# Eight small tiles placed in front of hhi and hlo, so that two activation tiles begin at another address

## The reference, cut to what matters

```python
h = rms_norm(x, norm1_w) * (1.0 + scale1) + shift1
proj = h @ w_in                                   # 1024 wide in: q, k, v, xBC, z, dt, gates
...
merged = g_attn * (attn @ w_attn_out) + g_ssd * (ssd @ w_ssd_out)
x = x + gate1 * (merged @ w_o)
h2 = rms_norm(x, norm2_w) * (1.0 + scale2) + shift2
x = x + gate2 * (square(relu(h2 @ w_mlp1)) @ w_mlp2)
# second block
u = rms_norm(h, norm1_w);  proj = u @ w_in
...
h = h + mix @ w_out
u2 = rms_norm(h, norm2_w)
h = h + (silu(u2 @ w_gate) * (u2 @ w_up)) @ w_down
```

## Time and profile before

| | |
|---|---|
| runs of the kernel before | 1010.43, 1007.97, 1009.35 us, median 1009.35 |
| profiled execution, span from the first to the last instruction | 1007.1 us |
| TensorE matmul busy, share of the span | 938.6 us, 93% |
| VectorE, ScalarE, GpSimd busy | 667.8, 511.2, 105.6 us |
| mean granted TensorE clock | 0.976 of full speed |
| bytes read from HBM | 166.73 MB, 167 GB/s over the span |

### The profile page before, as it was taken

How to read it: one execution, slowest core, us unless ns; L and a number is a source line. 1 busy time by engine, 2 the same in 40 slices (tenths; PEclk the granted TensorE clock), 3 DMA queues, 4 the chain that set the end, 5 groups by cost and what they waited for, 6 DMA issues and landing times.

```text
span 1007.1 us, 18347 instructions
## 1 busy us (share of the span) xinstructions
PE 938.6 (93%) x7516; PEld 904.7 (90%) x7516; DVE 667.8 (66%) x945; ACT 511.2 (51%) x696; POOL 105.6 (10%) x85
## 2 busy tenths in 40 slices
PE   4299999999987988998999999999998999999998
PEld 4299999888876878998999999989998989999998
DVE  5855899988489998775866644453675665555552
ACT  2365654666677666343545533344558544444431
POOL 0500155200124343000000000000000000000000
PEclk9999999999999999998999999989999989999999
DMA  9755344566411225474755555535241235555561
GB/s 344 271 202 187 126 168 162 212 212 209 169 58 68 84 85 187 172 263 172 251 189 171 197 183 193 177 124 190 85 156 54 93 120 190 184 175 201 176 209 35
DMA packets 25086, 168.81 MB, mean 168 GB/s; under 512 B 2868, under 2 KB 4532, under 8 KB 4920
## 3 DMA queue, kind: packets, MB, share of 16 engines
q1 hardware_dynamic: 23616, 164.64, 47.0%
q10 hardware_dynamic: 1400, 3.16, 0.8%
HBM read 166.73 MB, written 1.06 MB: 167 GB/s over the span
## 4 chain that ended last, share of the span: by engine, by line
PE 78%; DVE 8%; ACT 7%; issue 4%; POOL 1%; DMA 1%; POOLq 0%; SPq 0%; DVEq 0%; ACTq 0%
PE bank L1689 76%; ACT kw__113 L747 2%; DVE acc L1043 1%; DMA raw<-w_stream 1%; POOL sqs L467 1%; DVE wlo L1020 1%; ACT whi L532 1%; PE bank L1872 1%; DVE kw__113 L1292 1%; DVE eb L1283 1%; DVE hlo L1126 0%; DVE yt L1313 0%; DVE kw__113 L1299 0%; ACT zt L772 0%; ACT L724 0%
## 5 line engine op out<-in xcount | busy, mean ns | idle before, releaser
L1689 PE MATMUL bank<-hhi,whi 128*128 128x256 f32 (+1 forms) x1384 | 404.8, 292 | 11.9 <-DVE hlo L1126 6.8
L1020 DVE TENSOR_TENSOR wlo<-raw,whi 128x2048 fp32r<-128x2048 f32 (+1 forms) x131 | 300.6, 2295 | 159.3 <-ACT whi L532 159.1
L1689 PE MATMUL bank<-hlo,whi 128*128 128x256 f32 (+1 forms) x1384 | 397.3, 287 | 0.0
L1689 PE MATMUL bank<-hhi,wlo 128*128 128x256 f32 (+1 forms) x1384 | 397.1, 287 | 0.0
L532 ACT ACTIVATE whi<-raw 128x2048 fp32r<-128x2048 f32 (+1 forms) x132 | 250.2, 1896 | 90.6 <-PE bank L1689 65.5
L1689 PEld LDWEIGHTS bank<-hhi,whi 128*128 128x128 f32 (+1 forms) x1384 | 270.3, 195 | 19.6 <-issue 17.9
L1689 PEld LDWEIGHTS bank<-hlo,whi 128*128 128x128 f32 (+1 forms) x1384 | 270.7, 196 | 0.3
L1689 PEld LDWEIGHTS bank<-hhi,wlo 128*128 128x128 f32 (+1 forms) x1384 | 270.2, 195 | 0.0
L1689 PE MATMUL bank<-fhi,whi 128*128 128x256 f32 x432 | 121.1, 280 | 0.0
L1689 PE MATMUL bank<-fhi,wlo 128*128 128x256 f32 x432 | 120.5, 279 | 0.0
L1689 PE MATMUL bank<-flo,whi 128*128 128x256 f32 x432 | 120.5, 279 | 0.0
(11 more groups left out here) (274 smaller groups left out, 1293.1 us busy)
## 6 DMA issues: line engine op xcount, KB each, us to landing
raw<-w_stream SPq DMA_DIRECT2D x156, 1024.0 KB, 4.9
xres<-x_t ACTq DMA_DIRECT2D x1, 1024.0 KB, 10.0
out<-oute SPq DMA_DIRECT2D x8, 128.0 KB, 4.4
tabs<-tabs_in_dram ACTq DMA_DIRECT2D x1, 641.0 KB, 5.6
tabs<-tabs_in_dram ACTq DMA_DIRECT2D x1, 512.0 KB, 3.4
hankel<-bucket_rows ACTq DMA_DIRECT2D x1, 512.0 KB, 5.9
cols<-cols_in_dram ACTq DMA_DIRECT2D x1, 325.0 KB, 12.9
tabs<-tabs_in_dram ACTq DMA_DIRECT2D x1, 64.0 KB, 12.6
```

The lines of the kernel that those rows point to most:

```text
L1020: nc.vector.tensor_tensor(out=wlo[:, c % RING, 0:n], in0=raw[:, r % RING, 0:n], in1=whi[:, c % RING, 0:n].bitcast(f32), op=ALU.subtract)\
L1689: return nc.tensor.matmul(out, lhsT, rhs, start=start, stop=stop)
```

## The change

Eight small tiles (448 bytes of a partition together) stand in front of `hhi` in place of behind `tabs`. The diff is complete:

```diff
     raw = place("raw", [P, RING, CW], f32)
     whi = place("whi", [P, RING, CW], f32r)
     wlo = place("wlo", [P, RING, CW], f32r)
-    hhi = place("hhi", [P, KD, T], f32r)
-    hlo = place("hlo", [P, KD, T], f32r)
-    xres = place("xres", [P, KD, T], f32)
-    cols = place("cols", [P, NCOL], f32)
-    tabs0 = here[0]
-    tabs = place("tabs", [P, NTAB], f32)
     csil = place("csil", [P, KD], f32)
     mod = place("mod", [P, 48], f32)
     mscale = place("mscale", [P, 2 * KD], f32)
     root = place("root", [P, NT], f32)
     rcol = place("rcol", [P, NT], f32)
     qw8 = place("qw8", [P, 2], f32)
     epsc = place("epsc", [P, 1], f32)
     onec = place("onec", [P, 1], f32)
+    hhi = place("hhi", [P, KD, T], f32r)
+    hlo = place("hlo", [P, KD, T], f32r)
+    xres = place("xres", [P, KD, T], f32)
+    cols = place("cols", [P, NCOL], f32)
+    tabs0 = here[0]
+    tabs = place("tabs", [P, NTAB], f32)
     dtk = place("dtk", [P, NT, 2 * NH], f32)
```

## The result

The changed kernel took 991.55 us (median of four runs, 989.66 to 995.58), the kernel before 1009.15 us beside it (median of four runs, the fourth being 1008.96). The ratio is 0.9846, 95% interval 0.9817 to 0.9874: 17.6 us less, where 15.5 were forecast. The ratios here compare runs taken beside each other; the median of the kernel before differs from one set to the next (1006.59 to 1009.15 us).

What follows compares the result with a forecast made beforehand. TensorE, busy 93% of the span, was taken to bound the kernel by matmul spacing. Phase gains of 17.7 us, less 0.6 lost in m2 and 1.6 for waits and settling, gave 15.5 us: 1009.35 to 994 us, range 986 to 1004.

Steps and rivals of the forecast that it cites:

- The cause: Products streaming hhi or hlo: the streamed tile's address against the loaded weights sets the spacing, 120.0 against 113.3 or 117.8 ns.
- my slower rival: hhi at 576 modulo 1024, unlike the arena's 64, might lock at 122 ns: 1016 us; chance 0.05.
- The bounds of one product: Each hhi or hlo product on the chain gains 2.22 to 6.67 ns; 3,500 products give 7.8 to 23.3 us.
- Which of the two: How a series begins sets 113.3 or 117.8 ns until something interrupts; assigned by phase, the hhi gains sum to 17.7 us.
- one of my signs of being wrong: gu at 117.8 ns in the profile after: the entry rule, and with it the largest term, 6.9 us, would be wrong.
- the rival's 2.3: Slow arena spacing everywhere: all hhi products, gu included, at 117.8 ns; 1004.7 us, or 1002 if dn loses nothing; chance 0.17.
- The first term: First stretch (340 products) and z (336) begin behind many-column float32 matmuls: 113.3 ns, 4.5 us saved.
- m2 inherits: If m1 ends at 117.8 ns, m2's first 133 products probably stay there and lose 0.6 us.
- The other tiles cost nothing: Moving xres, cols and tabs costs nothing; if tabs mattered on some 300 matmuls, 1.8 us either way.
- a sign of being right: Profile after: hhi spacing 113.3 or 117.8 ns in m1 and gu, while ao, so and wo stay as before.
- What the saving meets: Other engines, tight VectorE in xbc (3.8 us slack) and settling runs take off 1.6 us; the weight stream has room.

Runs made afterwards that it cites:

- e2: Kernel before with dtk placed in front of hhi: hhi and hlo move 512 bytes but keep remainder 128 modulo 512; 1007.62 us, ratio 1.0005.
- e3: Changed kernel with raw, whi and wlo moved too, so weight rings, hhi, hlo and arena all begin at remainder 64; 1014.4 us, ratio 1.0072.
- e1: TensorE alone, both blocks left out: streamed pair at sixteen remainders, 0 to 480, weights at 128; 113.3 ns at 64, 120.0 at 128.
- e7: The changed kernel unaltered, run again on another chip run with a second profile; 988.54 us, ratio 0.9837, profiled execution 988.32 us.
- e4: Changed kernel with gsel and ngsel (64 bytes) between hhi and hlo: hhi stays at remainder 64, hlo at 128; 1003.43 us, ratio 0.9961.
- e8: Third placement, edited from the kernel before: wlo at remainder 0, hhi and hlo at 64 modulo 256, whi at 128; 980.95 us, ratio 0.9751.
- e5: TensorE alone, both blocks left out: streamed pair at remainders 32 to 92 in 4-byte steps, four entries each; only 64 reached 113.3 ns.
- e9: TensorE alone, both blocks left out: streamed pair at 64 or 192, wlo at 128 or 0, eleven entries each; 113.3 and 117.8 ns at the change's placement.
- e6: TensorE alone, both blocks left out: high tile, low tile and wlo at different remainders, 22 cases; 21 at 116.9 to 121.1 ns, one at 113.33.

## Why the prediction was right, step by step

**The cause: right, and sharper now.** I inferred from ao beside ga and gs that the streamed tile's address modulo 512 mattered relative to the weights. e2 and e3 show it: hhi at a new place but at distance 0 keeps 120.0 ns (e2), and dn, whose tile stays at its address while the weights move to distance 0, falls from 113.4 to 119.9 ns (e3). The period is 256 bytes (e1). "Modulo 1024", my slower rival, had no part: hhi at 576 behaves as fhi at 64.

The windows (e1, e3) show that a weight load and a streamed operand disturb each other by their addresses. The Trainium skill's page "SBUF — State Buffer", section "Who interferes with whom", has TensorE's two SBUF read ports independent and TensorE waiting on no one; by it none of these runs could differ. The measurement decides, and the spacing differs by 6% between distance 0 and the best. How the reads collide inside is not shown here.

**The bounds of one product: right.** 2.22 to 6.67 ns; in the long stretches with hhi nothing outside the arena's two spacings appeared. The parts that I then name add up to 3,559 products where the bounds use 3,500, which moves them by 0.1 and 0.4 us.

**Which of the two: wrong in part, and this was the uncertain term.** I had read the state off the kind of entry. It is not fixed by that: two executions of one program had gu in different states. I had expected 113.3 ns for gu because its clock rises within it. Three long stretches with hhi begin in this way, at 474, 667 and 816 us of before: in the first profile only the first of them was at 113.3 ns, in e7 all three. gu at 117.8 ns was one of my signs of being wrong, and the first profile shows it. Term by term, from the starts of the same matmuls in the profiles of before, of the change and of e7:

| stretch of before | forecast | first profile | e7 |
|---|---|---|---|
| 47 to 103 and 195 to 266 us | 4.5 | 1.3 | 1.1 |
| xbc, 103 to 172 us | 2.3 | 2.7 | 2.7 |
| 470 to 569.5 us (m1) and out2 | 1.9 | 2.7 and 0.5 | 2.4 and 1.1 |
| m2's first 15 us | -0.6 | -0.6 | -0.6 |
| in2, 673 to 752 us | 2.1 | 1.9 | 4.0 |
| gu | 6.9 | 2.3 | 6.9 |
| dn | 0 | -2.3 | 0.0 |
| sum | 17.1 | 8.5 | 17.6 |

gu's 6.9 us is exactly what e7 has, and the first profile has the rival's 2.3. m1 and xbc gained more than their terms, in2 in e7 alone, where about 0.8 of its 4.0 us is a shorter time at the lower clock. For m1 the reason is an oversight of mine: it is not one unbroken series. Eight one-column matmuls stand behind its fourth chunk, and the 192 products in front of them were at 113.3 ns, the 576 behind them at 117.8. The line of before:

```profile
499.53 0.95 PE L1689 MATMUL bank<-onec,acc 128*128 128x1 f32 x8
```

That the total came out close owes something to luck. The spans of the two profiles are 13.3 and 20.7 us shorter than that of before, and the table's stretches account for only 8.5 and 17.6 of them. The rest, 4.8 and 3.1 us, came from places where I had forecast nothing, and is told below. The medians are 17.6 and 19.0 us shorter than those beside them, the forecast was 15.5.

**The first term: sized too high.** I gave it 4.5 us and it brought 1.3 and 1.1. Some 190 products before 83 us went at 117.8 and not at 113.3 (0.8 us), z's runs of 24 gained 1.7 us in place of 2.2, and the clock took most of the rest. Windows from 95 to 104 us, of before and of the change:

```profile
95.00:104.00 9.00, 9.00 (x68) 0.81 0.27 107
```

```profile
95.00:104.00 9.00, 9.00 (x54) 0.62 0.24 97
```

The clock was at its lower level twice as long there (0.62 against 0.81 of full on the mean), which is 14 matmuls fewer in 9 us, 1.7 us. e7 has the same 0.62. Of the other placements e2, e4 and e8 have 0.81 as before, and e3 has 0.58. Whether this time belongs to the change is open. Over the whole span the mean granted clock of the first profile is the same as before, 0.976.

**m2 inherits: right. The other tiles cost nothing: wrong in part.** m2's start at 117.8 cost 0.6 us as worked out. I had not seen that the arena phases would change their states as well. m2 had 117.8 in all seven later stretches before. After, the stretches alternate, 113.3 in the first, third, fifth and seventh and 117.8 between them, alike in both profiles of the change. Windows of the first two, of the change:

```profile
578.30:588.30 10.00, 10.00 (x90) 1.00 0.60 211
590.00:600.00 10.00, 10.00 (x87) 1.00 0.62 210
```

This gave 1.4 us back, and the same in wo 0.4 us. ao alternates too, where all eight runs had been at 113.3, but it lies off the chain. I had named ao, so and wo staying as before as a sign of being right. In m2 the only tile that the change moved is `onec`, which the one-column matmuls between the stretches stream: from remainder 160 to 32 modulo 256. The profiles with onec at 160 and the weights at 128 (before, e2) have 117.8 in all seven, those with it at 32 (the change, e7, e4) alternate. So the move of onec is the likely cause; no run moved it alone.

The clock gave the rest, and that is not shown to come from the change. Between 774 and 789.5 us (attention of block 2) the granted clock was 0.89 before and 1.00 in both profiles of the change, 1.4 us. Another 1.6 us came around 400 us in the first profile. Windows of so's first matmuls, of before and of the change:

```profile
395.50:402.50 7.00, 7.00 (x49) 0.76 0.94 336
```

```profile
391.60:398.60 7.00, 7.00 (x63) 1.00 0.92 342
```

e7 has 0.76 there like before, with the same program as the first profile, so this part is luck of the execution. The runs of before beside e2 to e4 go from 1001.3 to 1010.6 us; that such differences of the clock make their spread is not shown.

**What the saving meets: right.** VectorE did not become the bound in xbc, the ring of three slots held gu at 113.3 ns, and 266 to 395 us is as long as before within 0.2 us. The other moved tiles cost VectorE and ScalarE nothing: VectorE's busy time is 667.2 against 667.8 us, ScalarE's 511.4 against 511.2.

## What to carry to other kernels

When the same product takes a different time from start to start with another tile, compare the addresses of its two operands, not the engines around it. Their addresses matter modulo 256 bytes, and every tile of the group must be at its place: here high and low activation at 64, whi at 128, wlo at 0. 4 bytes off, most or all of the gain is gone: 118.6 to 118.9 ns at 60 and 121.7 at 68, against 120.0 where nothing is moved and 113.3 at 64 (e5). Take more than one profile of such a kernel before a term is believed, since a phase of 1,000 matmuls may be in either of two states in the next execution. Follow every tile that a change moves, also those of the short matmuls between the long series.

## What the runs showed of the hardware that was not expected

- Three matmuls of 128 x 128 by 128 x 256 with their weight loads take 340, 353 or 360 ns in this kernel, by little more than the addresses of the tiles modulo 256 bytes; single remainders gave up to 370 ns (e5, 52).
- The spacing has two stable states at one placement, 113.33 and 117.78 ns. A state is kept across 1,500 products and across a change of the streamed tile (gu to dn), until another matmul breaks in. The same break may be followed by either, from one execution to the next (gu) or within one (e9), but in m2 the two alternated alike in both profiles of the change.
- With wlo at remainder 0 and both streamed tiles at 64, none of 20 series of e9, none of three of e6 and no long stretch of the whole kernel was at 117.78 ns. Why this placement and none of the other six moves of wlo gives 113.33 ns stays open, as does the rule by which the three reads add up: neither of the two simple ones fits e4 and e6.
